# Order of the attention units: one sequence after the other, with three small jobs moved to other units

## The reference, cut to what matters

```python
h = x @ w_in                                   # q | k | v | fourier
q, k, v, f = jnp.split(h, [...], axis=-1)
def one_block(args):                           # per 128-query block i
    k_blk = lax.dynamic_slice_in_dim(kp, start, nkeys, axis=1)   # nkeys = 3 * 128
    logits = einsum('bqkgd,bjkd->bkgqj', q_blk, k_blk) * scale + bias
    logits = jnp.where(valid, logits, -jnp.inf)
    m = jnp.maximum(jnp.max(logits, axis=-1), sink_f)
    p = jnp.exp(logits - m[..., None])
    probs = p / (jnp.sum(p, axis=-1) + jnp.exp(sink_f - m))[..., None]
    out = einsum('bkgqj,bjkd->bqkgd', probs, v_blk)
mix = jnp.concatenate([rms_norm(attn, g_attn), rms_norm(four, g_four)], axis=-1) @ w_o
x = layer_norm(ALPHA * x + mix, ln1_g, ln1_b)
x = layer_norm(ALPHA * x + conv_ffn(x, ...), ln2_g, ln2_b)
```

## Time and profile before

| What | Value |
| --- | --- |
| Device time, median of 3 runs (lowest, highest) | 983.73 us (983.41, 983.89) |
| The profiled execution: device time | 982.7 us |
| The profiled execution: span of the trace | 980.9 us |
| Mean granted clock of PE | 0.997 |
| PE busy, share of the span | 98% |
| PEld | 81% |
| DVE | 81% |
| ACT | 50% |
| POOL | 28% |

### The profile page before, as it was taken

One profiled execution on the slowest core, in us unless ns is written; L12 is line 12 of the kernel. 1 busy time (PEld: TensorE's weight loads), 2 busy tenths in 40 slices (PEclk: granted clock), 3 DMA queues, 4 the chain that ended last, 5 costly groups with the idle time before them and its releaser, 6 DMA issues.

```text
span 980.9 us, 12198 instructions
## 1 busy us (share of the span) xinstructions
PE 959.3 (98%) x4442; PEld 795.1 (81%) x4442; DVE 793.8 (81%) x1164; ACT 494.3 (50%) x756; POOL 275.0 (28%) x254
## 2 busy tenths in 40 slices
PE   7999998999999999999999999999999999999996
PEld 6888887788888788888888888888888878888885
DVE  6665567887696699988888888898978669997698
ACT  6574666897503565445445545544555555333200
POOL 2400425785770000001100100100000199790022
PEclk9999999999999999999999999999999999999999
DMA  8335143906431214464553644554526885564212
GB/s 313 99 73 164 26 126 107 321 2 178 166 129 43 86 54 102 125 171 101 136 164 83 161 132 116 148 140 118 136 82 236 340 344 191 194 237 177 104 65 108
DMA packets 110811, 142.21 MB, mean 145 GB/s; under 512 B 21163, under 2 KB 72319, under 8 KB 110752
## 3 DMA queue, kind: packets, MB, share of 16 engines
q1 hardware_dynamic: 104352, 129.82, 39.6%
q0 software_dynamic: 5184, 9.44, 6.9%
q10 hardware_dynamic: 1216, 2.17, 0.7%
HBM read 112.32 MB, written 47.97 MB: 163 GB/s over the span
## 4 chain that ended last, share of the span: by engine, by line
PE 84%; DVE 7%; ACT 4%; issue 2%; DMA 2%; POOL 0%; DVEq 0%; SPq 0%; ACTq 0%; POOLq 0%
PE ps L781 27%; PE ps L783 27%; PE ps L782 27%; ACT prob L2044 2%; DMA db_raw<-in_w_down 2%; DVE prob L1476 1%; DVE pTl L1269 1%; DVE bn L1272 1%; ACT pTh L1866 1%; DVE acc L1839 1%; DVE acc L1820 1%; PE ps L1125 1%; PE ps L816 1%; DVE db_lo L1269 0%; DMA acc<-in_x_prompt 0%
## 5 line engine op out<-in xcount | busy, mean ns | idle before, releaser
L781 PE MATMUL ps<-db_hi,ga_hi 128*128 128x512 f32 x252 | 98.3, 390 | 1.4 <-DVE db_lo L1269 1.0
L783 PE MATMUL ps<-db_hi,ga_lo 128*128 128x512 f32 x252 | 98.1, 389 | 0.0
L782 PE MATMUL ps<-db_lo,ga_hi 128*128 128x512 f32 x252 | 98.1, 389 | 0.0
L781 PE MATMUL ps<-x1h,wa_hi 128*128 128x512 f32 x192 | 75.6, 394 | 0.0
L2164 ACT ACTIVATE hc<-U,taps 128x512 f32<-128x512 f32 x60 | 48.7, 813 | 53.3 <-DVE U L1655 41.4
L783 PE MATMUL ps<-x1h,w_lo 128*128 128x512 f32 x192 | 74.8, 389 | 0.0
L782 PE MATMUL ps<-x1l,wa_hi 128*128 128x512 f32 x192 | 74.7, 389 | 0.0
L1866 ACT ACTIVATE ga_hi<-ga_raw 128x1536 fp32r<-128x1536 f32 x21 | 31.3, 1490 | 67.3 <-DMA db_raw<-in_w_down 35.1
L2169 ACT ACTIVATE hc<-hc 128x512 f32<-128x512 f32 x44 | 27.9, 633 | 70.8 <-DVE hc L1672 70.8
L1269 DVE TENSOR_TENSOR ga_lo<-ga_raw,ga_hi 128x1536 fp32r<-128x1536 f32 x21 | 47.9, 2283 | 16.7 <-ACT ga_hi L1866 16.7
L726 POOL TENSOR_TENSOR acc<-acc,gain_bc 128x1024 f32<-128x1024 f32 x12 | 37.9, 3161 | 84.0 <-ACT bias_bc L1866 84.0
(11 more groups left out here) (317 smaller groups left out, 2988.1 us busy)
## 6 DMA issues: line engine op xcount, KB each, us to landing
w_raw<-in_w_up SPq DMA_DIRECT2D x44, 512.0 KB, 4.8
ga_raw<-gs_scratch SPq DMA_DIRECT2D x21, 768.0 KB, 4.5
ts_scratch<-in_w_down SPq DMA_DIRECT2D x12, 768.0 KB, 14.5
gs_scratch<-gsum SPq DMA_DIRECT2D x9, 1024.0 KB, 4.6
db_raw<-ts_scratch SPq DMA_DIRECT2D x12, 768.0 KB, 5.9
db_raw<-in_w_down SPq DMA_DIRECT2D x9, 768.0 KB, 7.4
ts_scratch<-in_w_down POOLq DMA_DIRECT2D x18, 256.0 KB, 5.0
gs_scratch<-gated SPq DMA_DIRECT2D x9, 512.0 KB
```

Of the source, the lines that this page charges most:

```text
L781: pe.matmul(out, whi, xhi, start=start, stop=False, skip_group_check=onto)
L782: pe.matmul(out, whi, xlo, start=False, stop=False, skip_group_check=onto)
L783: return pe.matmul(out, wlo, xhi, start=False, stop=stop, skip_group_check=onto)
```

## The change

The pairs are reordered so that all eight units of the first sequence come ahead of those of the second: the widths of the 16 units, in key blocks, were 2 2 3 3 2 2 3 3 3 3 3 3 2 2 2 2 and become 2 2 3 3 3 3 2 2 2 2 3 3 3 3 2 2. The waits for the second sequence's queries and keys move from unit 4 to unit 8. `WO_UNITS` becomes (6, 7, 8, 9). On DVE `proj_low(11)` goes from the start of step 1 to the end of its logits, and `zero_keys(1)` from ahead of step 0 to step 4, between the last logits and the last `probs_low`. On ACT `proj_high(11)` goes from the start of step 1 to behind its second exponential. PE's, POOL's and SP's programs keep their order but for the units' new order. The whole diff:

```diff
--- before.py
+++ after.py
@@ -57,7 +57,7 @@
 
 
 
-PAIRS = ((0, 0), (1, 0), (0, 1), (1, 1), (2, 0), (2, 1), (3, 0), (3, 1))
+PAIRS = ((0, 0), (1, 0), (2, 0), (3, 0), (0, 1), (1, 1), (2, 1), (3, 1))
 
 
 def unit(n):
@@ -69,7 +69,7 @@
 STAT_BLOCKS, NORM_BLOCKS = (2, 4, 5, 6), (3, 5, 6, 7)
 
 
-WO_UNITS = (3, 4, 10, 12)
+WO_UNITS = (6, 7, 8, 9)
 
 
 def key_blocks(blk):
@@ -974,7 +974,7 @@
                         pe.wait_ge(f_lo, 16)
                         pe.wait_ge(qk_lo, 6)
                         pe.wait_ge(kz_zero, 4)
-                    elif n == 4:
+                    elif n == 8:
                         pe.wait_ge(qk_lo, 12)
                         pe.wait_ge(kz_zero, 8)
                 if s >= 3:
@@ -1503,15 +1503,16 @@
             proj_low(10)
             logits(1, 2)
             logits(1, 3)
-            zero_keys(1)
             dve.wait_ge(ss_ps, 1)
             dve.tensor_scalar(vf[:], ps[:, 6, 0:TT], 1.0 / (FG * P), EPS, ALU.mult, ALU.add).then_inc(var_mix, 1)
             for n in range(UNITS):
-                if n == 1:
-                    proj_low(11)
                 for j in range(GRP):
                     if n + 2 < UNITS:
                         logits(n + 2, j)
+                    if n == 1 and j == 3:
+                        proj_low(11)
+                    if n == 4 and j == 3:
+                        zero_keys(1)
                     if j == 1 and n >= 4 and n % 2 == 0:
                         attn_low(n // 2 - 2)
                     if j == 1 and n - 1 in WO_UNITS:
@@ -2073,11 +2074,11 @@
             exp(1, 2)
             exp(1, 3)
             for n in range(UNITS):
-                if n == 1:
-                    proj_high(11)
                 for j in range(GRP):
                     if n + 2 < UNITS:
                         exp(n + 2, j)
+                    if n == 1 and j == 1:
+                        proj_high(11)
                     if j < len(key_blocks(unit(n)[0])):
                         probs_high(n, j)
                 if n >= 3 and n % 2:
```

## The result

The changed kernel takes 985.91 us (median of 17 runs, 984.85 to 987.01), the kernel before beside it 983.41 (17 runs, 982.48 to 984.94). The ratio is 1.0024, with a 95% interval of 1.0017 to 1.0031: slower by 2.4 us. (The ratios given here are those on record; they differ from the quotients of the medians beside them by up to 0.0004.) The profiled execution of the changed kernel took 986.48, with a span of 984.7, against 982.7 and 980.9 before. That is 3.8 more, not 2.4.

The account below looks back on a forecast made before the run. The chain of DVE and ACT was taken to bound the loop. Step 13 starts 1.5 us later; PE reaches the output projection +1.4, unit 13's values add +0.7: +2.1 on the profiled execution, median 985.8, range 981.5 to 988.0.

Parts of the forecast that it names:

- Slower by over 0.2%: Whole kernel: the case that the changed kernel loses more than 0.2%, about 2 us; chance 0.51.
- The chain of ACT and DVE: Attention loop: DVE and ACT hand work to and fro; a step costs its width's time plus ACT's lateness.
- Zero keys ahead of step 0: DVE before the loop: without the four instructions, first logits start at 157.8 in place of 158.95, -1.1 us.
- The last query tile: Steps 0 to 2: its ACT and DVE jobs stay in the chain; step 2 starts at 169.5, before 170.93.
- Zero keys in step 4: DVE, between fourth logits and third low part: 1.9 us less a wait of 0.2, +1.7; bounds 0 and 1.9.
- Splits behind steps 6 to 9: ACT: with mah behind 7 and 9, steps 7 to 10 late by 0.70, 1.53, 0.70 and 1.66 us.
- The values of unit 13: PE behind the output projection's start: nine matmuls in place of six, +0.7 us.
- The cover taken at nothing: POOL's normalising, least room in steps 6 and 7: counted as nothing, some tenths each if the cover went.
- The clock: PE's new pauses in steps 2 and 5: low clock behind them counted as 0, with +0.6 us each as bound.
- PE as the bound: Loop: PE's waits and slow stretch set the time, so 979.6 us, or 981.8 with step 5's pause; chance 0.20.
- Low clock behind every pause: PE at steps 2, 5 and 8 to 10: up to 0.6 us each, +1.2 to +2.4, 987.0 to 988.2; chance 0.15.
- Moved work mostly covered: Zero keys cost 0.9, or mah and split 0.5 less in steps 8 and 10: about 984.5 us; chance 0.17.

Follow-up runs that it names:

- The splits at even steps: Kernel before with the four weight splits behind steps 2, 6, 8 and 10 in place of 3, 4, 10 and 12: 981.68 us, ratio 0.9984.
- the filled pause: Changed kernel with nine extra matmuls on PE in the pause of step 5, their values read by nothing: 985.32 us, ratio 1.0024.
- the new order with its jobs placed by the rule: Changed kernel with splits behind steps 2, 4, 10, 12 and the four zero-key instructions one by one in steps 2 to 5: 983.46 us, ratio 0.9999.

## Why the prediction was right

**The end.** Forecast 985.8, measured 985.91; +2.1 forecast on the profiled execution, +2.5 by the medians. "Slower by over 0.2%" had 0.51, and the ratio is 1.0024, with an interval that reaches down to 1.0017. So the side is well supported, and that it lies beyond 0.2% is only likely. That the number is right to 0.1 is in part luck: I counted 2.1 on a median of 983.73, and measured are 2.5 on 983.41.

**What bounds the kernel.** The chain of ACT and DVE, step by step. The profile taken again shows it best, as it has no slow stretch:

| Term | Forecast | Changed kernel again |
| --- | --- | --- |
| step 4 (narrow logits, mah ahead, zero keys in it) | 4.49 + 0.34 + 1.7 = 6.53 | 6.70 |
| step 5 | 4.49 | 4.49 |
| step 6 | 3.65 + 0.22 = 3.87 | 3.87 |
| step 7 | 3.65 + 0.70 = 4.35 | 4.36 |
| step 8 | 4.14 + 1.53 = 5.67 | 5.69 |
| step 9 | 4.14 + 0.70 = 4.84 | 4.83 |
| step 10 | 4.97 + 1.66 = 6.63 | 6.62 |
| steps 11 and 12 | 4.97 and 4.83 | 4.97 and 4.84 |
| logits of step 13 to first matmul on woh0F | 3.4 | 3.39 |

That matmul starts at 229.81 in this profile, forecast 229.0: 0.3 of the difference lies ahead of the loop, 0.3 in steps 0 and 1, 0.2 in step 4. In the profile shown first it starts at 230.98, with 0.7 ahead of the loop and 0.8 of low clock (1.0 in step 5, 0.2 back in step 7).

**Zero keys ahead of step 0.** Forecast -1.1. The first logits come at 158.49, and take away the 0.7 by which all was late ahead of them (the previous query tile's instruction on DVE starts at 155.24, before at 154.59), so 157.8, as forecast.

**The last query tile.** "The wait is not gone, it is spread" was right, and even the 0.3 that I gave the move was too much: with the zero keys moved as well it is worth 0. The reading that failed is that ACT's instruction waits for the projection on PE. The projection was done by 162.85; what released ACT was its own last exponential, which ends at 163.99, when the tile starts. From the timeline of ACT in the kernel before:

```profile
163.37 0.62 ACT L2044 ACTIVATE prob<-prob,negm 128x385 f32<-128x385 f32 x1 [0.43 <-DVE negm L1476]
```

So the tile's start goes with the logits. That reading also made my expectation for the tile in its old place too slow by 0.8. Step 2 starts 0.3 later than I had added up (170.48 less the 0.7 ahead of the loop is 169.8, forecast 169.5).

**Zero keys in step 4.** Forecast +1.7 with bounds of 0 and 1.9; measured 1.85. I let DVE wait 0.2 there; the upper bound was nearly the truth. The wait of PE behind it was forecast at about 2.2 and is 2.1.

**Splits behind steps 6 to 9.** The lateness in steps 7 to 10 is right to 0.03, but the attribution was not. Forecast, the splits' new places cost 1.9 against their old ones; undoing the move gives back 1.3 by the steps and 0.8 by the ratios. The missing term is POOL's buffer: without the splits, steps 8 and 10 are late anyway (5.31 and 6.32, where the forecast's terms give 5.04 and 6.01), which is the 0.6 between 1.9 and 1.3. In the changed kernel ACT comes so late that POOL's sum is always done, so one lateness hides the other, and leaving the term out did no harm to this sum. It did harm to the expectation for the order alone: 0.7 of the 1.1 by which it was off.

**The values of unit 13.** Forecast +0.7. From the first matmul on woh0F to the one behind those values it takes 236.65 - 230.98 = 5.67, before 232.74 - 227.62 = 5.12: +0.55.

**The cover taken at nothing.** POOL's cover for the probabilities held: steps 6 and 7 came at the forecast cost. The cover that I had not named, POOL giving back `sqa`, didn't hold for the order alone.

**The clock.** I took 0 and kept 0.6 as a bound for each new pause. In step 2 it was 0; in step 5 it was 0 in one profile and 1.0 in the other, beyond the bound, and filling the pause left the median where it was. The bound was too small because I looked at the wrong wait. I counted 1.4 of cover for the transposes that ACT wants, but what gave way was DVE's first logits of step 6, which wait for PE's scores. PE was late by 1.6 there, the step by 1.0, so the cover was some 0.6.

The Trainium skill (TensorE: Matmul & The Clock Gate, HAM oscillation) says that a PE which idles between bursts falls back to the low clock; the kernel it tells this of has longer waits, for DMA, that come back in every round. Here the clock fell behind the 2.09 us of one profile and not behind the 2.10 us of the next, and behind the 2.37 of before but not behind the 2.37 of the order alone, so for pauses of this size it is a risk and no rule.

**The rivals.** PE as the bound would have put the time at 979.6 or 981.8. Three kernels speak against it. The splits at even steps leave PE's work and its longest wait as they are and win 1.5; the zero keys at their old place win as much and move only work of DVE; and POOL's sum put first takes 0.7 out of two steps. The kernel with the query tile at its old place says less, since it only trades PE's waits of 1.14 and 1.03 in step 2 for 1.80 in step 1, and the filled pause says nothing on this. Low clock behind every pause: not in the median; and three or four times the 0.6 would be 1.8 to 2.4, not from 1.2 on. Moved work mostly covered: no, 1.85 of 1.9 and, behind step 6, 0.7 of a split's 0.7 were paid.

**Why the change costs, added up.** By the ratios: order alone +1.1, the zero keys' move +1.5, the splits' move +0.8, the query tile 0. That is 3.4 where 2.5 are measured, but each ratio is good to about 0.9 us only, and the parts were taken from different kernels. The profiles are sharper. The loop takes:

| Kernel | The loop takes |
| --- | --- |
| before | 73.03 |
| order alone | 73.13 |
| order alone, squares summed first | 72.40 |
| changed, zero keys at their old place | 73.65 |
| changed, query tile at its old place | 74.99 |
| changed (the profile without a slow stretch) | 74.94 |

One part after the other: the order +0.10, with the +0.7 of POOL's buffer in it; the splits' new places +1.12 (steps 3 to 12 of the kernel with the zero keys at their old place, against the order alone); the query tile's new place -0.60 (steps 0 to 2 of the same two); the zero keys' new place +1.29, which is 1.85 in step 4 less what they cost ahead of step 0. That makes 1.91, and with the 0.55 of unit 13's values 2.46, as the medians have it. The tile's -0.60 is what the sum of the ratios misses: taken back out of the whole, where the zero keys' move has already moved the tile, it shows as 0.

## What to carry to other kernels

Where two engines hand work to and fro in program order, a job moved into the chain is paid in full (1.85 of 1.9 here), and a wait that disappears from the list of waits may have become chain: ask of each moved job whether the engine is free at its new place, step by step, and not whether some engine waits less. A split on ACT cost 0.7 behind a step with two transposes and next to nothing behind one with three; two fillers in one wait of DVE were one too many; and the third engine that gives back a single buffer belongs in the sum. A part's worth also depends on which of the other parts are in: the query tile's move was worth 0.6 without the zero keys' and 0 with it. The same two jobs, moved to steps where the engines had room, won 2.3 us here (ratio 0.9977), and 3.4 (3.1 by the medians) with a third.

## What the runs showed that I had not expected

- A pause of PE of 2.1 us is followed by a low clock in some executions and not in others of the same kernel (mean granted clock 0.62 and 1.00 over the same four us). The same holds for the wait of 2.4 in step 1: 0.72 over 168 to 174 before, 1.00 in the three kernels that have a wait of 2.36 or 2.37 there (the order alone, the same with the squares first, the splits at even steps). In the new order with its jobs placed by the rule, pauses of only 1.14 and 1.03 were followed by 0.69, and the same two pauses in the changed kernel by 1.00. A single profile must not be taken for the kernel here: it overstated the loss by 0.8 us.
- An instruction of 0.42 to 0.48 us put into DVE's wait for ACT costs next to nothing if it is alone there (0.05 and 0.01), and up to 0.7 if the low half of a split (0.87 us) stands in the same wait.
- Nine extra matmuls of 128 x 512 (2.32 us) put into a pause of PE cost nothing in the median (985.32 against 985.33).
